# Pooling output product: a fourth block-product group per column pair, with two or one plain units between groups

## What is computed

```python
def pool_mixer(xn, w_in, w_group, scale, w_out):
    ...
    mixed = jnp.einsum('bsgc,gcd->bsgd', pooled, w_group).reshape(B, S, E_POOL)
    return (mixed * scale * jax.nn.silu(g)) @ w_out

def first_block(...):
    ...
        h = h + rms_norm(out, post_norm[i])
        gate = jax.nn.sigmoid(rms_norm(h, ple_norm[i]) @ ple_w_gate[i])
        h = h + (p[i] @ ple_w_proj[i]) * gate
```

## Time and profile before

| | |
|---|---|
| median of 3 runs | 2434.01 us (2433.85 to 2434.53) |
| the profiled execution | 2434.6 us, of which the span from first to last instruction is 2432.7 us |
| PE busy | 2422.3 us |
| DVE busy, ACT busy, POOL busy | 1717.1 us, 1381.2 us, 82.9 us |
| TensorE clock granted | 0.999 of full speed, mean |
| chain that ended last | PE 99%, DVE 1% |
| HBM | 186 GB/s over the span |

### The profile page before, as it was taken

One profiled execution on the slowest core, in us unless ns is written; L12 is line 12 of the kernel. 1 busy time (PEld: TensorE's weight loads), 2 busy tenths in 40 slices (PEclk: granted clock), 3 DMA queues, 4 the chain that ended last, 5 costly groups with the idle time before them and its releaser, 6 DMA issues.

```text
span 2432.7 us, 34024 instructions
## 1 busy us (share of the span) xinstructions
PE 2422.3 (100%) x12667; PEld 2082.3 (86%) x12667; DVE 1717.1 (71%) x2080; ACT 1381.2 (57%) x1830; POOL 82.9 (3%) x100
## 2 busy tenths in 40 slices
PE   9999999999999999999999999999999999999998
PEld 8888888888889999878888888888988888888887
DVE  7675757788765656786656767665666666679997
ACT  6444444556656666565755556565645545556655
POOL 0000000001100000010000000000000000000001
PEclk9999999999999999999999999999999999999999
DMA  8666666676556554575585564454566666657785
GB/s 314 197 188 187 189 184 187 194 242 215 183 178 182 173 164 141 211 229 195 163 234 169 155 178 144 165 181 154 175 186 180 188 191 180 189 172 212 239 234 162
DMA packets 237363, 462.46 MB, mean 190 GB/s; under 512 B 15265, under 2 KB 60753, under 8 KB 236220
## 3 DMA queue, kind: packets, MB, share of 16 engines
q1 hardware_dynamic: 230960, 435.94, 57.6%
q0 software_dynamic: 5888, 24.34, 3.9%
q10 hardware_dynamic: 396, 0.59, 0.2%
HBM read 448.68 MB, written 2.69 MB: 186 GB/s over the span
## 4 chain that ended last, share of the span: by engine, by line
PE 99%; DVE 1%; ACT 0%; issue 0%; ACTq 0%; DVEq 0%
PE ps L835 25%; PE ps L837 13%; PE ps L801 12%; PE ps L803 12%; PE ps L802 12%; PE ps L985 6%; PE ps L986 6%; PE ps L987 6%; PE ps L759 1%; PE ps L866 1%; PE ps L867 1%; PE ps L868 1%; PE ps L1473 1%; PE ps L1244 0%; PE ps L1232 0%; PE ps L1431 0%
## 5 line engine op out<-in xcount | busy, mean ns | idle before, releaser
L2468 DVE TENSOR_TENSOR w_lo<-raw,w_hi 128x1024 fp32r<-128x1024 f32 x689 | 842.1, 1228 | 466.7 <-ACT w_hi L1643 446.5
L1643 ACT ACTIVATE w_hi<-raw 128x1024 fp32r<-128x1024 f32 x689 | 726.9, 1060 | 651.7 <-PE ps L837 358.8
L835 PE MATMUL ps<-x_hi_lo,w_hi 128*128 128x512 f32 x2336 | 821.5, 394 | 0.0
L837 PE MATMUL ps<-x_hi_lo,w_lo 128*128 128x256 f32 x2336 | 661.0, 283 | 0.0
L835 PEld LDWEIGHTS ps<-x_hi_lo,w_hi 128*128 128x128 f32 x2336 | 439.1, 188 | 101.3
L801 PE MATMUL ps<-w_hi,x_hi_lo 128*128 128x512 f32 (+3 forms) x1184 | 461.9, 390 | 0.0
L803 PE MATMUL ps<-w_hi,x_hi_lo 128*128 128x512 f32 (+3 forms) x1184 | 453.7, 383 | 0.0
L802 PE MATMUL ps<-w_lo,x_hi_lo 128*128 128x512 f32 (+3 forms) x1184 | 452.7, 382 | 0.0
L837 PEld LDWEIGHTS ps<-x_hi_lo,w_lo 128*128 128x128 f32 x2336 | 439.5, 188 | 0.0
L1820 ACT ACTIVATE w_hi<-raw 128x1024 fp32r<-128x1024 f32 x207 | 215.6, 1052 | 159.7 <-PE ps L987 136.7
L2476 DVE TENSOR_TENSOR w_lo<-raw,w_hi 128x1024 fp32r<-128x1024 f32 x207 | 248.9, 1222 | 34.7 <-ACT w_hi L1820 34.5
(11 more groups left out here) (469 smaller groups left out, 2732.6 us busy)
## 6 DMA issues: line engine op xcount, KB each, us to landing
raw<-in_w_up SPq DMA_DIRECT2D x160, 512.0 KB, 4.2
raw<-in_pool_w_in SPq DMA_DIRECT2D x126, 512.0 KB, 3.9
raw<-in_w_in SPq DMA_DIRECT2D x96, 480.0 KB, 4.0
raw<-in_w_down SPq DMA_DIRECT2D x84, 512.0 KB, 5.5
raw<-in_pool_w_out SPq DMA_DIRECT2D x64, 512.0 KB, 5.0
raw<-in_ple_w_gate SPq DMA_DIRECT2D x64, 512.0 KB, 4.3
raw<-in_mla_w_in SPq DMA_DIRECT2D x56, 448.0 KB, 3.6
raw<-in_pool_w_group SPq DMA_DIRECT2D x32, 512.0 KB, 4.1
```

Of the source, the lines that this page charges most:

```text
L835: pe.matmul(bank, w_hi[:, slot, cols], xs[:, k].rearrange("p s n -> p (s n)"), start=k == 0, stop=False, skip_group_check=True)
L837: last = pe.matmul(bank[:, 0:T], w_lo[:, slot, cols], xs[:, k, 0, :], start=False, stop=k == nkt - 1, skip_group_check=True)
L1643: act.activation(w_hi[:, t.slot(), :], raw[:, slot, :], ACT.Copy).then_inc(S("w_hi"), 1)
L2468: dve.tensor_tensor(w_lo[:, t.slot(), :], raw[:, u % RAW, :], w_hi[:, t.slot(), :].bitcast(F32), ALU.subtract)\
```

## The change

In the pooling output product 16 row tiles are plain and 16 in four groups. Pair 0 has nine plain units, a group (n = 9), two plain, a group (12), two plain, a group (15), one plain, a group (17) and two plain. Pair 1 has four plain units, a group (4), two plain, a group (7), two plain, a group (10), one plain, a group (12) and seven plain. The sums on the side of `y` are a third longer (1024 in place of 768 numbers for a partition), the piece of `y` ahead of them is four tiles in place of eight, and one more piece is split behind them. Entries of `n` move with the list: the later splits of `y`, the combination of pair 0's banks (now at n = 18, 19 and after the list), ACT's squares of chunk 2 (n = 19 in place of 22). `columns_out` of chunk 2 comes behind the list, and `rope_angles` between the first and the second of the three splits for proj0. The buffers of the rope constants move to make room for the longer sums.

```diff
--- before.py
+++ after.py
@@ -85,12 +85,12 @@
     return [[(part, n, k) for part in PARTS] for n, k in enumerate(first_tiles)]
 
 
-POOL_QUADS = [20, 24, 28]
-P0, P1, P2, P3 = ([plain(c, (k, k + 1)) for k in range(0, 20, 2)] for c in range(NCH))
+POOL_QUADS = [16, 20, 24, 28]
+P0, P1, P2, P3 = ([plain(c, (k, k + 1)) for k in range(0, 16, 2)] for c in range(NCH))
 PQ = quads_at(POOL_QUADS)
-POOL_OUT = [P0[:9] + P1[:1] + PQ[:1] + P1[1:4] + PQ[1:2] + P1[4:7] + PQ[2:] + P1[7:] + P0[9:],
-            P2[:4] + PQ[:1] + P2[4:7] + PQ[1:2] + P2[7:9] + P3[:1] + PQ[2:] + P2[9:] + P3[1:]]
-POOL_Y = [(0, 4), (4, 8), (8, 12), (12, 20), (20, 24), "sums", (24, 28), (28, 32)]
+POOL_OUT = [P0[:8] + P1[:1] + PQ[:1] + P1[1:3] + PQ[1:2] + P1[3:5] + PQ[2:3] + P1[5:6] + PQ[3:] + P1[6:],
+            P2[:4] + PQ[:1] + P2[4:6] + PQ[1:2] + P2[6:8] + PQ[2:3] + P3[:1] + PQ[3:] + P3[1:]]
+POOL_Y = [(0, 4), (4, 8), (8, 12), (12, 16), (16, 20), "sums", (20, 24), (24, 28), (28, 32)]
 DOWN_QUADS = [20, 24, 28, 32, 36]
 DOWN_WHOLE = [tuple(range(k, min(k + 2, FKT))) for k in (*range(0, 20, 2), 40, 42)]
 D0, D1, D2, D3 = ([plain(c, kts) for kts in DOWN_WHOLE] for c in range(NCH))
@@ -378,12 +378,12 @@
     MLG = [arena(f"mla_logits{n}", 105984 + 1536 * n, [128, 384]) for n in range(3)]
     MPT = [arena(f"mla_p_T{n}", 110592 + 1536 * n, [128, 3, 128]) for n in range(2)]
     mnmx, mpsm, mprc = (arena(f"mla_{n}", 113664 + 32 * k, [128, 4, 2]) for k, n in enumerate(("neg_max", "prob_sum", "prob_scale")))
-    posi = arena("positions", 112640, [128, 2], I32)
-    posf = arena("positions_f", 112672, [128, 2])
-    freqs = arena("rope_freq", 112704, [128, 32])
-    ang = arena("angle", 112896, [128, 2, 32])
-    turns_ = arena("angle_turns", 113152, [128, 2, 32])
-    red = arena("angle_reduced", 113408, [128, 2, 32])
+    posi = arena("positions", 115488, [128, 2], I32)
+    posf = arena("positions_f", 115520, [128, 2])
+    freqs = arena("rope_freq", 115552, [128, 32])
+    ang = arena("angle", 115744, [128, 2, 32])
+    turns_ = arena("angle_turns", 116000, [128, 2, 32])
+    red = arena("angle_reduced", 116256, [128, 2, 32])
 
     KVM = 115456 - 512
     memt = arena("mem_tokens", 32768, [128, 2, D])
@@ -499,8 +499,8 @@
     FSUMS = 32768 - 6 * 1024 * nq
     fsums, fsums_lo = (arena(name, FSUMS, [128, 3, nq, 2, 128], dt) for name, dt in (("ffn_y_sums", F32), ("ffn_y_sums_lo", F32R)))
     fsums_hi = [arena(f"ffn_y_sums_hi{n}", FSUMS + (3 + n) * 1024 * nq, [128, nq, 2, 128], F32R) for n in range(3)]
-    psums, psums_lo = (arena(name, 81920, [128, 3, 3, 2, 128], dt) for name, dt in (("pool_y_sums", F32), ("pool_y_sums_lo", F32R)))
-    psums_hi = [arena(f"pool_y_sums_hi{n}", off, [128, 3, 2, 128], F32R) for n, off in enumerate((91136, 94208, 106496))]
+    psums, psums_lo = (arena(name, 81920, [128, 3, 4, 2, 128], dt) for name, dt in (("pool_y_sums", F32), ("pool_y_sums_lo", F32R)))
+    psums_hi = [arena(f"pool_y_sums_hi{n}", off, [128, 4, 2, 128], F32R) for n, off in enumerate((94208, 106496, 110592))]
     dsum = arena("down_sum", 120832, [128, 512])
     pool_out = Paired("pool_out", y32, yh, yl, POOL_Y, psums, psums_hi, psums_lo, POOL_QUADS, POOL_STEPS, POOL_LOADS,
                       POOL_QUADS_END, POOL_PLAIN_END, 0, POOL_SUMS)
@@ -1940,8 +1940,8 @@
                 for m in range(3):
                     last = act.activation(psums_hi[m], psums[:, m], ACT.Copy)
                 last.then_inc(S("y_hi"), 1)
-            if n in (10, 11):
-                y_hi(n - 4)
+            if n in (9, 12, 14):
+                y_hi(n // 3 + 3 if n < 14 else 8)
         for n, entry in enumerate(pool_out.steps[1]):
             step_hi(entry)
             if n == 15:
@@ -1951,7 +1951,7 @@
             if n == 13:
                 act.wait_ge(S("gains_in"), 16)
                 split_p(0)
-            if n == 22:
+            if n == 19:
                 square_mixed(2)
         hi(2)
         act.wait_ge(S("rope_reduced"), 2)
@@ -2939,10 +2939,10 @@
                 dve.wait_ge(S("y_done"), 2 * WB + 4)
             if n in (7, 8):
                 y_lo(n - 3)
-            if n in (10, 11):
-                y_lo(n - 4)
-            if n in (21, 22):
-                quads_mixed(0, n - 21)
+            if n in (10, 13, 15):
+                y_lo(n // 3 + 3)
+            if n in (18, 19):
+                quads_mixed(0, n - 18)
         for n in (2, 3):
             quads_mixed(0, n)
         for n, entry in enumerate(pool_out.steps[1]):
@@ -2955,11 +2955,10 @@
                 split_p()
             if 16 <= n <= 19:
                 quads_mixed(1, n - 16)
-            if n == 20:
-                columns_out(pool_out, outt, 2)
-            if n == 21:
-                rope_angles()
-        lo(3)
+        columns_out(pool_out, outt, 2)
+        lo(1)
+        rope_angles()
+        lo(2)
         t.add("chunk", 4)
         columns_out(pool_out, outt, 3)
         layer_end(0, 1, "pool_out", GAIN["pre1"])
```

## The result

| | before | after |
|---|---|---|
| median of the runs, us | 2434.05 (2433.34 to 2434.92) | 2437.72 (2437.33 to 2438.43) |
| profiled execution, its own time, us | 2434.6 | 2437.7 |
| its span, us | 2432.7 | 2435.9 |
| start of the product on PE, us | 458.29 | 457.66 |
| end of the product on PE (E), us | 629.18 | 628.45 |

There are 22 runs of each. The ratio is 1.0016, with a 95% interval of 1.001 to 1.0021: 0.15% slower, 3.7 us. That is clear of the scatter of the runs, but within the 0.2% that counts as no change. Twelve matmuls fewer, and no time won.

A forecast was written before the change was run, and what follows sets the result against it. PE, fed almost without a gap, was taken as the bound, with DVE's work behind it deciding. Matmuls -2.8, pair 0 +3.4, tail +2.2 and POOL +0.2 gave +3.0 on 2434.0: 2437.0 us, range 2433.3 to 2439.8.

The forecast's parts named there:

- What is removed: In the pooling output product, twelve matmuls go, 732 to 720, which takes 2.80 us off PE if it stays fed.
- Pair 0: In the product's first half, DVE's splits come late for PE, 3.5 us in sum, less 0.1 us of today's slips.
- the walk: Following DVE's queue operation by operation against PE's needs; each late unit taken as known within 0.1 to 0.2 us.
- the seam: Where pair 1 follows pair 0: its first unit waits for bank combinations and its split, late by 0.4 us.
- Pair 1 at nothing: In the product's second half, no late unit and no cost; the closest, T2, is 0.6 us early in every group.
- The end of the product: On PE, net of the removed matmuls, the product ends 0.6 us later than before.
- The tail: Behind the product, `columns_out` of the last chunk comes 2.2 us later, paid by PE, plus 0.2 us for POOL.
- POOL beside DVE: Behind the product, POOL's multiplication of chunk 2 slows proj0's first split and `rope_angles`: 0.2 us, ends 0 and 0.6.
- POOL's queue: Rival, chance 0.09: loads stretched by half delay the second group's DMA sum, making T1 4.8 us late: 2441.8 us.
- DVE stands still for POOL: Rival, chance 0.05: DVE cannot run beside POOL's gain of chunk 2, 2.0 us per operation: 2438.8 or 2440.8 us.
- Covered ring: Rival, chance 0.05: the ring of four buffers covers DVE, no gap opens, all 2.8 us come: 2431.2 us.
- one cost only: Rival, chance 0.15: only pair 0's lateness is paid, 2434.6 us, or only the tail's, 2433.6 us.

The follow-up runs named there:

- control run: The kernel before the change (three groups in each pair), with only `rope_angles` moved into the mixer: 2433.66 us, ratio 0.9999.
- first `rope_angles` experiment: The changed kernel with `rope_angles` moved from between the splits of proj0's first two units to n = 15 of pair 1: 2439.01 us, ratio 1.0021.
- `rope_angles` in the mixer: The changed kernel with `rope_angles` done 300 us earlier, in the second turn of the pooling groups: 2434.46 us.
- `rope_angles` twice: The changed kernel with `rope_angles` done twice in a row at its place, ACT waiting for the second: 2440.8 us.
- `y` moved: The changed kernel with the three late splits of `y` at n = 10, 13 and 14 on both ACT and DVE: 2436.07 us.

## Why the prediction was right, and where it wasn't

- *What is removed.* 720 matmuls, as said, 2.8 us. Right.
- *Pair 0.* The seven late places are those of the walk (splits by DVE that come late): B21, T2 and the plain unit of the first group (0.5, 0.7, 0.3 forecast; 0.39, 0.72, 0.33 measured), behind the second group (0.3; 0.33), behind group 15 (0.7; 0.70), T2 of group 17 (0.5; 0.54), the seam (0.4; 0.45). The sum was 3.5 us and is 3.46. Three groups in pair 0 instead of four take all seven away, and moving `y` takes most of the later ones, so it is this queue. How the 1.1 us of the first group divide between the sums and the missing plain unit is argued from the walk only.
- *Pair 1 at nothing.* Right: no wait, though four groups stand there.
- *The end of the product.* 0.6 us later was forecast. It is 0.1 us shorter (170.79 against 170.89). The late units are all there, but the matmuls of this execution start 0.2325 us apart where those of the execution before did 0.2333, which over 720 is 0.6 us. The step that failed is that I took the pace of one trace as fixed. Against the control run, which has the product of before at the usual pace (170.34 us), the product is 0.45 us longer, close to the 0.6.
- *The tail.* +2.4 us forecast, +3.48 measured. The term that was mis-sized is POOL beside DVE: 0.2 us with an end of 0.6, from the split at 622.13 of the earlier trace rows, and it was 1.1 us through DVE and 0.2 through the clock, for which the sum had no term. I read that row as a split that ran through beside POOL. It had begun when POOL's first operation, from 620.79 to 622.58, had 0.45 us left, ended 0.3 us late, and POOL's second operation took 2.28 us in place of 1.30, for it waited for the split in turn. So the row shows a nearly finished wait and not the price of one. The CAST came just when POOL's second operation was starting its work. With POOL's operation made small, `columns_out` came at E + 2.4, so the walk itself (2.2 us) was right.
- *Where PE waits in the tail.* The prediction takes the 0.3 us lost at 634.95 for the 0.6 us wait of the earlier trace rows. It is not: that wait lies in the second gated embedding, by this row of before, and none is listed at 634.95. The 0.3 us come from the starts and stand.

```profile
1087.78 0.50 PE L801 MATMUL ps<-w_hi,ple_hi 128*128 128x512 f32 x1 [0.63 <-ACT ple_proj L1740]
```

For the new kernel I named proj0's third unit. It was already the second, for DVE's `mixer_out`: this unit writes the banks that `columns_out` reads. I had only looked at the read-out, and of two waits that move together the earlier one shows. The sum isn't changed by that, for the third unit ends it either way: the read-out is 4.35 us behind `columns_out` (4.38 forecast), and 636.38 + 1.23 = 637.6 us is where PE could go on. The half clock that the gap brought made it 637.8, counted as above from the next matmul.
- *POOL's queue.* POOL issued the second group's DMA sum at 482.03, and no wait of PE's in front of T1 names a DMA. This rival fell.
- *DVE stands still for POOL.* I gave it 0.05, and its mechanism came true, its size not. For these operations the two engines take turns, a whole operation at a time, both ways. In the changed kernel the CAST was held by 1.1 us, in the first `rope_angles` experiment four small operations by 4.1 us together, and with `rope_angles` in the mixer a full-size split took 2.31 us. An operation of POOL's takes 1.30 us alone (control run, at 620.13); the 2.0 us each of the earlier trace rows already held waits for DVE. So 2.0 us was too much for one hold, and 0.2 too little. In a sentence apart: the Trainium skill (SBUF — State Buffer, "SBUF: two separate sides") says that of GpSimd's operation and a VectorE operation that has two SBUF inputs or runs in a 2-port mode, whichever starts first holds the shared ports for the whole instruction, and counts cast and tensor_scalar among those that can run so. The trace agrees: the held operations are splits with two SBUF inputs (1.22 us alone, 2.31 held), a CAST (0.16, 1.26) and TENSOR_SCALARs (0.20, 1.22).
- *The median.* 2437.0 us forecast, 2437.72 measured. Two errors of about 1.1 and 0.7 us had opposite signs in the trace: tail too small, product too long. The product also began 0.6 us earlier, and what follows gate 0's first matmul took 0.4 us more, neither of which was forecast. That the profiled execution is met to 0.1 us (2437.6 forecast, 2437.7 measured) is luck. With the tail alone right the median would have been forecast as 2438.1, 0.4 us too high, and this 0.4 stays open.
- *Covered ring, one cost only.* Both fell: the two costs are there, and they add.

Open: the 1.1 us of the first group, which no experiment took away with four groups in pair 0; why the pace is 0.2333 us in some stretches (the same matmuls ran at both, so the kernel does not decide it); 0.8 us of `rope_angles` twice.

## What to carry to other kernels

When matmuls are traded for vector work, walk the queue of the vector engine past each gap and past the end of the product, and place small helpers that depend on nothing (here `rope_angles`) where no gap hangs on them: that placement cost more than the change could win. A kernel whose PE waits for almost nothing still pays for each later row on DVE one for one. Before pricing one engine beside another from a row, look how long the other engine's operation still had to run in that row, and whether that operation got longer too. And look which of two waits on the same chain comes first.

## What the runs showed of the hardware

- Splits, CASTs and TENSOR_SCALARs on DVE and POOL's TENSOR_TENSOR of 128x512 take turns, whatever their size: the later one is held until about the end of the other. On DVE: CAST of 128x2, 0.16 us alone, 1.26 beside it (changed kernel, `rope_angles` early); TENSOR_SCALAR of 128x64, 0.20 and 1.22; split of 128x1024, 1.22 and 2.31 (`rope_angles` in the mixer). `rope_angles` as a whole 2.53 us, 3.63 and 6.66. On POOL: 1.30 us alone, 2.27 to 2.29 when a split was running at its start. Not held were DVE operations that read PSUM banks and at most one SBUF buffer, and a RECIPROCAL: in the kernel before a COPY at 605.02 and a TENSOR_TENSOR at 607.26, each of 128x512, took 0.68 us beside POOL, and in the changed kernel a RECIPROCAL of 128x2 at 636.51 took 0.17.
- A gap of 2.35 us from start to start on PE, after a long stretch without one, was followed 1.1 us later by a granted clock of 0.51 (1.2 GHz) for 3.1 us, with matmuls 0.43 us apart. After gaps of 2.33 us (`y` moved) and 2.32 us (three groups in pair 0) the same pace of 0.43 us began 0.4 and 0.7 us after the restart. After a gap of 4.87 us PE came back at half clock at once, for 2.7 us. After gaps of 1.63, 1.73 and 1.50 us (`rope_angles` early) the clock did not fall.
- The pace of the same matmuls in fed stretches was 0.2333 us for most of the product in two executions (before, POOL's operation made small) and 0.2323 to 0.2326 in the others, at a granted clock of 1.00 either way. In the trace of before it was 0.2326 from 460 to 500 us, 0.2333 from 500 to 620 and 0.2324 from 660 to 700. Over 720 matmuls that is 0.6 us, about the size of the effects looked for here.
